# Delta rule by head pairs on partitions, key norms in exponents, and x by column pairs at the front

## What is computed

```python
q = l2norm(silu(conv(u Wq))) * HEAD_DIM ** -0.5;  k = l2norm(silu(conv(u Wk)));  v = silu(conv(u Wv))
beta = sigmoid(b);  g = cumsum within a chunk of -exp(A_log) * softplus(a + dt_bias)
decay[i, j] = exp(g_i - g_j) for j <= i, else 0
lower = strict_lower((k * beta) @ k.T * decay);  system = lower + I          # 64 x 64, per head and chunk
u_vals, w_keys = solve(system, [v * beta, k * beta * exp(g)])
qk = (q @ k.T) * decay;  k_tail = k * exp(g_last - g);  q_head = q * exp(g)
for each chunk:                                                               # the scan
    v_new = u_vals - w_keys @ state
    out   = q_head @ state + qk @ v_new
    state = state * exp(g_last) + k_tail.T @ v_new
o = rmsnorm(out, out_norm) * silu(z)
```

## Time and profile before

| | us |
|---|---|
| median of 3 runs | 2066.68 (2061.85 to 2067.53) |
| profiled execution | 2068.45 |
| its span, first to last instruction | 2066.1 |
| mean granted TensorE clock | 0.985 |
| TensorE busy | 2009.2 |
| VectorE, ScalarE, GpSimd busy | 920.4, 775.1, 437.4 |

### The profile page before, as it was taken

The page is one execution under the profiler, slowest core; times in us unless marked ns, Lnnn a source line. Parts: engine busy times, 40 slices in busy tenths (PEclk is TensorE's granted clock), DMA queues, the critical chain, the costliest instruction groups (busy, mean ns, idle before and its releaser), DMA issues.

```text
span 2066.1 us, 24221 instructions
## 1 busy us (share of the span) xinstructions
PE 2009.2 (97%) x9416; PEld 1650.8 (80%) x9416; DVE 920.4 (45%) x862; ACT 775.1 (38%) x860; POOL 437.4 (21%) x295
## 2 busy tenths in 40 slices
PE   7999999999999799999999999999999999999998
PEld 5888888877778588888888888888887778888886
DVE  6544333378753354334335343333336554433323
ACT  4432222267343344434224244333224444443221
POOL 3312220114912132112101011122011032211111
PEclk9999999999998899999999999999999999999999
DMA  5343323342220123333233433332343133333231
GB/s 164 102 122 102 102 70 98 107 161 80 62 61 18 61 82 102 102 102 87 76 108 106 153 110 85 100 102 70 98 122 148 42 82 102 89 93 95 84 98 69
DMA packets 331021, 197.11 MB, mean 95 GB/s; under 512 B 18575, under 2 KB 327968, under 8 KB 330322
## 3 DMA queue, kind: packets, MB, share of 16 engines
q1 hardware_dynamic: 325648, 182.54, 31.0%
q10 hardware_dynamic: 4418, 10.59, 1.4%
q0 software_dynamic: 896, 3.16, 0.4%
HBM read 189.80 MB, written 6.46 MB: 95 GB/s over the span
## 4 chain that ended last, share of the span: by engine, by line
PE 91%; DVE 4%; ACT 2%; DMA 1%; POOL 1%; issue 0%; SPq 0%; ACTq 0%; DVEq 0%; POOLq 0%
PE ps L580 28%; PE ps L582 28%; PE ps L581 28%; PE ps L747 1%; DVE w_lo L1675 1%; PE ps L972 1%; PE ps L977 1%; PE ps L994 1%; DMA raw<-in_ffn_w_gate_up 1%; PE ps L987 1%; PE ps L1136 1%; PE ps L1162 0%; PE ps L761 0%; POOL sq L2348 0%; ACT w_hi L1243 0%
## 5 line engine op out<-in xcount | busy, mean ns | idle before, releaser
L580 PE MATMUL ps<-x_hi,w_hi 128*128 128x512 f32 x1792 | 710.9, 397 | 7.5 <-DVE x_lo L1681 5.9
L582 PE MATMUL ps<-x_hi,w_lo 128*128 128x512 f32 x1792 | 698.8, 390 | 0.0
L581 PE MATMUL ps<-x_lo,w_hi 128*128 128x512 f32 x1792 | 698.6, 390 | 0.0
L1243 ACT ACTIVATE w_hi<-raw 128x2048 fp32r<-128x2048 f32 (+1 forms) x186 | 320.6, 1724 | 775.9 <-PE ps L582 775.9
L1675 DVE TENSOR_TENSOR w_lo<-raw,w_hi 128x2048 fp32r<-128x2048 f32 (+1 forms) x186 | 407.5, 2191 | 211.9 <-ACT w_hi L1243 211.9
L580 PEld LDWEIGHTS ps<-x_hi,w_hi 128*128 128x128 f32 x1792 | 337.5, 188 | 83.1 <-issue 11.7
L582 PEld LDWEIGHTS ps<-x_hi,w_lo 128*128 128x128 f32 x1792 | 337.0, 188 | 70.9
L581 PEld LDWEIGHTS ps<-x_lo,w_hi 128*128 128x128 f32 x1792 | 337.5, 188 | 70.3 <-issue 2.9
L582 PE MATMUL ps<-hid_hi,w_lo 128*128 128x512 f32 x704 | 273.9, 389 | 0.0
L580 PE MATMUL ps<-hid_hi,w_hi 128*128 128x512 f32 x704 | 273.9, 389 | 0.0
L581 PE MATMUL ps<-hid_lo,w_hi 128*128 128x512 f32 x704 | 273.9, 389 | 0.0
(11 more groups left out here) (296 smaller groups left out, 1597.7 us busy)
## 6 DMA issues: line engine op xcount, KB each, us to landing
raw<-in_ffn_w_gate_up SPq DMA_DIRECT2D x176, 512.0 KB, 5.0
raw<-in_ffn_w_down SPq DMA_DIRECT2D x64, 384.0 KB, 3.9
raw<-in_ffn_w_down SPq DMA_DIRECT2D x64, 320.0 KB, 3.2
raw<-in_gdn_w_in SPq DMA_DIRECT2D x26, 512.0 KB, 4.7
raw<-in_w_out SPq DMA_DIRECT2D x16, 512.0 KB, 4.5
raw<-in_kv_w SPq DMA_DIRECT2D x12, 512.0 KB, 4.9
raw<-in_mem_w_kv SPq DMA_DIRECT2D x8, 512.0 KB, 4.2
raw<-in_fox_w_in SPq DMA_DIRECT2D x8, 512.0 KB, 4.5
```

Source lines behind the costliest of these rows:

```text
L580: nc.tensor.matmul(dst, hi, xh, start=first, stop=False)
L581: nc.tensor.matmul(dst, hi, xl, start=False, stop=False)
L582: return nc.tensor.matmul(dst, lo, xh, start=False, stop=last)
L1243: nc.scalar.activation(w_hi[s][:, 0:n], raw[s][:, 0:n], ACT.Copy).then_inc(hi_ready, 1)
```

## The change

At the front, SyncE loads the 16 rows of the first norm's gains, then x by pairs of column blocks, with the first weight unit in two halves between them, each with its own semaphore; TensorE turns a column pair when it is there, two ahead. The other gains and the conv table are turned behind unit 0, and the memory tokens are asked for in the middle of the first stage.

In the mixer, the two heads of a pair m lie side by side: head e on partitions 64 e to 64 e + 63, chunks in columns, so each product is made only for its 64x64 or 64x128 block, twice, on the two halves of the array (`own(e)`). Decay, lower and the solve are 24 blocks of 64 columns in three heads' worth of space, not six. Keys stay unscaled: the gram's diagonal gives the squared key lengths (`key_norms`), whose logarithm goes into the exponents of decay and gates. Query lengths are left out of q and come back as the epsilon of the output norm (`query_norm`, `query_eps`). Values and keys are turned to tokens by products with the identity in three groups of all chunks, and value and key products are finished beside the projections. The scan keeps only its four groups per chunk, with outputs of tokens on partitions, whose squares ScalarE sums; a transposition per chunk (`turn_output`) brings them back two chunks later. `round_hi(u + 15)` stands ahead of the scan, `cut_lo(u + 15)` in the last chunk behind `v_new`. The DMA wait of W_out's second unit for the key products is gone.

```diff
+                    first_w = raw[0][:].rearrange("p (k g n) -> p k g n", k=KT, g=2)
+                    half = KT // 2
+
+                    def load_x(i):
+                        cols = slice(2 * i * P, (2 * i + 2) * P)
+                        sp.dma_start(x_tok[:, :, cols], x_rows[:, :, cols]).then_inc(x_in[i], 16)
+
+                    sp.dma_start(first_rows[0:FIRST_GAINS, :],
+                                 ffn1_norm.rearrange("a (r c) -> (a r) c", c=P)).then_inc(first_gains_in, 16)
+                    load_x(0)
+                    for gu in (0, 1):
+                        sp.dma_start(first_w[:, 0:half, gu, :],
+                                     ffn_gu[0][:, 0:half, gu * FFN:gu * FFN + P]).then_inc(first_half_in, 16)
+                    load_x(1)
+                    load_x(2)
+                    for gu in (0, 1):
+                        sp.dma_start(first_w[:, half:, gu, :],
+                                     ffn_gu[0][:, half:, gu * FFN:gu * FFN + P]).then_inc(raw_in[0], 16)
+                    load_x(3)
...
-                    pe.wait_ge(gains_in, 16 * 7)
-                    nc.tensor.transpose(ps[:, 0, 0:GAINS], gain_rows[0:GAINS, :], ident[0:GAINS, 0:GAINS]).then_inc(table_tr, 1)
-                    pe.wait_ge(conv_in_sem, 16)
-                    nc.tensor.transpose(ps[:, 2, 0:4 * 18], conv_rows[0:72, :], ident[0:72, 0:72]).then_inc(table_tr, 1)
-                    pe.wait_ge(x_in, 16 * TT)
-                    for c in range(4):
-                        turn_x(c)
+                    pe.wait_ge(first_gains_in, 16)
+                    nc.tensor.transpose(ps[:, 2, 0:FIRST_GAINS], first_rows[0:FIRST_GAINS, :],
+                                        ident[0:FIRST_GAINS, 0:FIRST_GAINS]).then_inc(table_tr, 1)
+                    turn_x(0)
+                    turn_x(1)
                 elif name == "up0":
...
+                    def gram_product():
+
+                        pe.wait_ge(act_ready, len(K_UNITS))
+                        pe.wait_ge(cols_ready, 2)
+                        for m in range(HEAD_PAIRS):
+                            for n in range(CHUNKS):
+                                for e in range(2):
+                                    keys = k[:, 2 * m + e, chunk_cols(n)]
+                                    last = nc.tensor.matmul(ps[own(e), 4 + m, chunk_cols(n)], keys, keys,
+                                                            start=True, stop=True)
+                        last.then_inc(gram, 1)
+
+                    def query_norm(m):
+
+                        pe.wait_ge(q_squared, m + 1)
+                        for n in range(CHUNKS):
+                            for e in range(2):
+                                at = m * CHUNKS + n
+                                last = nc.tensor.matmul(ps[own(e), 7, at:at + 1], q_square[m % 2][:, e, chunk_cols(n)],
+                                                        ones[:, 0:1], start=True, stop=True)
+                        last.then_inc(q_norm, 1)
+
...
+                    def turn_tokens(m, src, b, signal):
+
+                        for n in range(CHUNKS):
+                            for e in range(2):
+                                last = nc.tensor.matmul(ps[own(e), b + n // 4, head_cols(n % 4)],
+                                                        src[:, 2 * m + e, chunk_cols(n)], ident[:],
+                                                        start=True, stop=True)
                         last.then_inc(signal, 1)
...
+                    def key_product(m):
+
+                        if m == 0:
+                            pe.wait_ge(low_scaled, 3)
+                            pe.wait_ge(k_tok_ready, HEAD_PAIRS)
+                        else:
+                            pe.wait_ge(w_ready, m)
+                        for n in range(CHUNKS):
+                            for e in range(2):
+                                last = nc.tensor.matmul(ps[:, by + e, chunk_cols(n)], k_tok[own(e), m, n, :],
+                                                        low[own(e), m, chunk_cols(n)], start=True, stop=True)
                         last.then_inc(w_prod, 1)
...
                     def beside(n, s):
 
-                        if n in range(3, 9) and s == 2:
-                            sum_squares(n - 2)
-                        if n == 3 and s == 5:
+                        if n == 3 and s == 2:
                             turn_gates()
-                        if n == 6 and s >= 4:
-                            gram_product(s - 4)
-                        if n == 9 and s >= 4:
-                            query_product(s - 4)
+                        if n == 5 and s == 2:
+                            gram_product()
+                        if n in (7, 8, 9) and s == 2:
+                            query_norm(n - 7)
+                        if n == 9 and s == 4:
+                            query_product()
                         if n == 11:
-                            if s in (3, 6, 9, 12):
-                                turn_values(s // 3 - 1)
-                            if s == 5:
-                                pe.wait_ge(qk_ready, TT)
+                            if s in (1, 3, 5):
+                                turn_values(s // 2)
+                            if s == 8:
+                                pe.wait_ge(v_tok_ready, 2)
                                 mem_scores(0, 0, q_mem)
+                            if s == 11:
+                                edges()
                             if s == 14:
-                                mem_turn(0, 0, 0)
+                                corners()
                         if n == 12:
                             if s == 0:
+                                mem_turn(0, 0, 0)
+                            if s == 2:
                                 mem_turn(0, 0, 1)
-                            if s == 3:
+                            if s in (3, 6, 9):
+                                value_product(s // 3 - 1)
+                            if s == 5:
                                 mem_values(0, 0, 4, mpt)
-                            if s == 7:
+                            if s == 8:
                                 pe.wait_ge(ma_out, 1)
                                 mem_scores(0, 1, q_mem)
-                            if s == 10:
-                                edges()
+                            if s in (11, 13, 15):
+                                turn_keys((s - 11) // 2)
                         if n == 13:
                             if s == 0:
                                 mem_turn(0, 1, 0)
-                            if s == 2:
-                                corners()
+                            if s in (2, 5, 8):
+                                key_product(s // 3)
                             if s == 3:
                                 mem_turn(0, 1, 1)
                             if s == 6:
                                 mem_values(0, 1, 4, mpt)
-                            if s == 7:
-                                turn_keys(0)
-                            if s == 11:
-                                value_product(0)
-                            if s == 13:
-                                key_product(0)
 
                     for n in range(Z_UNITS[0]):
                         unit(u + n, g + n, x_hi, x_lo, outs=1 if n == 0 else 2,
@@ -934,72 +953,58 @@
                                     last.then_inc((z_tile_done, unit_done)[o], 1)
                                 beside(n, KT * o + c)
...
+                        tok, st, ob = chunk_cols(n), state[n % 2], 4 + n % 2
                         for x in range(2):
                             if n == 0:
                                 continue
                             pe.wait_ge(state_ready, 2 * (n - 1) + x + 1)
-                            for hd in heads_in(x):
-                                last = nc.tensor.matmul(at_head(x, hd)[rows], k[:, hd, tok], st[:, hd, :],
-                                                        start=True, stop=True)
+                            for i, m in enumerate(SETS[x]):
+                                for e in range(2):
+                                    last = nc.tensor.matmul(ps[own(e), sb[x], head_cols(2 + i)], k[:, 2 * m + e, tok],
+                                                            st[:, 2 * m + e, :], start=True, stop=True)
                             last.then_inc(ws_prod, 1)
-                            pe.wait_ge(q_head_ready, p + 1)
-                            for hd in heads_in(x):
-                                nc.tensor.matmul(at_head(ob + x, hd)[:, rows], st[:, hd, :], q[:, hd, tok],
-                                                 start=hd % HALF_HEADS == 0, stop=False)
-                        if c == 1 and p:
-                            output_sum(p - 1)
+                        if n >= 2:
+                            pe.wait_ge(o_copied, n - 1)
+                        if n:
```

(70 more changed lines are left out.)

875 lines of the change are left out of this document (404 added, 471 removed).

## The result

The changed kernel takes 2009.28 us, the median of four runs (2008.01 to 2009.69), against 2067.05 (2061.85 to 2067.53) for the kernel before in the same series: a ratio of 0.9721, 95% interval 0.9708 to 0.9735, so 57.8 us less. The forecast was 2021 with a range of 2000 to 2042: the sign and the range held, the drop was forecast 12 us too small. The profiled execution took 2009.69 with a span of 2007.8.

The account below looks back on a forecast made before the run. TensorE, busy 97% of the span, was taken as the bound. Terms -7.3 + 11.5 - 43 - 6.5 = -45.3 on the profiled 2068.45 gave 2023, less 1.8 over the median: 2021 us, range 2000 to 2042.

Parts of the forecast that it names:

- Front: Kernel start: x by column pairs and half weight units bring the first product to 11.9, 7.3 us earlier; bounds 4 to 9.
- keeps its pace: Front: work behind the first product, with two column blocks of lookahead instead of four, was claimed not to slow.
- Beside the projections: Projections before the scan: products added and removed, waits and clock gone, new waits and solve delay; together +11.5 us.
- products added, less 28 removed: Projections: 42.5 us of new paired small products against 28 us removed, +14.5 us; bounds -2 and +25.
- solve, `token_values`, `mem_scores`: Before the scan: triangular solve back at about 567, TensorE there at 563, so a 4.5 us wait (0 to 10).
- Scan: Chunk scan: 3.7 us a chunk at full clock against 9.25, partly at half clock; 37 us for 80, -43.
- rival (a): Scan: clock stays full, 26 us in place of 37, time 2010; chance 0.22.
- 20 us at this level, as long as it lasted before: Scan: 20 us run at the 1.2 GHz level, the rest at the full clock.
- Rival (b): Scan: clock at 1.2 GHz throughout, 46.5 us and a tail of 13, +12.5, time 2033; chance 0.20.
- rival (c): New paired products: column halves work one after another, 0.107 us a record, time 2063, no change; chance 0.08.
- Rival (d): New paired products: every change between halves costs 0.17 us, 544 matmuls, +93, time 2114; chance 0.05.
- Tail: From the last `v_new` to the first `g` column: about 10 us against 16.8, -6.5 us.

Follow-up runs that it names:

- e_storage: Changed kernel with the triangular solve's blocks moved from under the token values to where the turned memory weights come later; 2011.0 us, ratio 0.9718.
- e_stall_once: Changed kernel with 12 copies of 512 columns on VectorE ahead of `v_new` of chunk 3, stalling TensorE in the scan; 2017.9 us, one run.
- b_dense: Kernel before the change, with 24 unused fp32r products of 128x128 by 512 columns ahead of the scan's first product; 2064.9 us, ratio 0.9991.
- after_again: The changed kernel itself, unaltered, run once more beside the later experiments; 2008.9 us, ratio 0.972.

## Why the prediction was right, and where it missed

**Front, -7.3 against -4.6.** The first product was forecast at 11.9 and came at 12.01. The failed step is the sentence that the work behind it "keeps its pace", with the reason that VectorE's copy and `x_lo` set it and not the transposes: the first unit became 2.6 us longer, because VectorE waits for transposes (2.25 us once, 0.53 once) for which it never waited in the first unit before.

**Beside the projections, +11.5 against +9.2.** By its terms, with what the trace after shows:

| term | forecast | measured |
|---|---|---|
| products added, less 28 removed | +14.5 | +8.9: 18 groups take 34.9 in all, and the product behind each 0.11 more |
| waits for squares | -8.5 | -8.5 |
| half clock before | -4 | -4.4: half of 3.5 and 5.4 busy us |
| half clock after | 0 | +2.7: half of 5.44 busy us |
| wait at unit 7 | +5 | +1.5 |
| solve, `token_values`, `mem_scores` | +4.5 | +9.6 |

These sum to 9.8, 0.6 more than the landmarks; the 28 removed are the forecast's own figure. Records cost 0.059 (0.053 taken); the gram and query products 0.031 in place of 0.040, norms 0.034 in place of 0.053 (3.3 us for 96 records). The three key products were taken at 2.7 each, for which the prediction gives no working; by its own 0.053 and 0.4 a group of 32 records is 2.1, and 2.1 is what one costs. The place of the new wait was named rightly, and half its size was forecast. The forecast had the inverse back at 567 and TensorE there at 563. The chain ran earlier (in e_storage, where the edges wait for it, the inverse is there at 560.8), but TensorE's wait began at 547, at the memory scores, and not at the edges. The step that went wrong is "`token_values` waits for the spill, and `mem_scores` for that": it was named, and then priced by the edges' due time. In the chain of the earlier trace rows GpSimd had L2 work between; without it the substitution took 51.7 us from 497.0 to 548.7.

**Scan, -43 against -54.** The chunk was forecast at 3.7 us and measured 3.61. All of the difference is the clock: rival (a), at 26 us for the scan, is what happened (26.8). The assumption taken over from the old scan, "20 us at this level, as long as it lasted before", was the failed term, of 10 us. Rival (b) did not come, and e_stall_once shows more: even when the clock is taken from the new scan it is back after one chunk. Why the old scan went without it for 18 us and the new one does not stays open. Here the Trainium skill's rule about overlap of weight loads (TensorE: Matmul & The Clock Gate, Part 3, The mechanism) was weighed as support of rival (c); the rows at L812, two column halves of the same rows, show 0.059 a record side by side and 0.10 in line, so the trace does not agree with it for short pairs. Rival (d), a drain at each change between halves, falls with the same rows.

**Tail, -6.5 against -6.6.** As forecast: 10 us taken, 10.1 measured, with VectorE's cut of the last unit's weights (2.55 us) in its path.

**The rest.** 2.4 us were not in the sum: the kernel before still ran at half clock until about 719, behind the last landmark. The sum had ended at 714.

Taken together, 10 of the 13 us between forecast and profile are the clock in the scan; the other terms missed by 2 to 3 us each and partly cancelled. The 2009.3 measured is rival (a)'s 2010, to which the prediction gave 0.22, and not the forecast, to which it gave 0.42; the range held because it had been drawn to take (a) in. That (a) comes so close is in part luck: the products beside the projections cost 5.6 us less than forecast, while the front gave 2.7 less, the two new waits took 1.6 more, and 2.7 at half clock were in no sum.

## What to carry to other kernels

Two small matmuls on different halves of the array nearly overlap (0.059 us a record against 0.10) if they stand next to each other in the queue; the order of a loop decides it. A DMA that is ready early can still be late behind another in the same queue that waits for a slot: look where it is issued and not when its data is ready, 7.2 us here. When a wait is removed and reappears at the next consumer with the same length, the producer is late, and the order of the consumers is the second thing to mend and not the first.

## What was not expected of the hardware

The clock stayed at 1.00 with TensorE busy for 73% of 25.8 us in waits of 1.1 to 1.7 us, and at the old scan's end in b_dense it fell with TensorE busy throughout. Runs of two matmuls on one half in a row cost nothing (12 records in 0.81 and 0.88 us in either order), runs of three cost 0.27 us a group. Short pieces of half clock come in some executions of a kernel and not in others (0.72 on average from 658 to 664 in after_again, 1.00 in the first profile of the same kernel, behind a wait of 1.9 us in both), about 2 us each. The recorded clock is not always the pace: at the front of the kernel after it reads 1.00 from 12.01 to 14.90, yet the first six products start 0.43 to 0.56 us apart, as in the kernel before at a recorded 0.50 from 19.20 to 22.00; at full clock they start 0.23 apart.
